# First phase's page scores behind the decay sums, four value sets in the last projection, and the first norm's last tiles in banks and a buffer of their own

## The chip, the cores and the metric

One core of a Trainium2 chip runs the whole program: one inference step of a two-layer decoder trunk. The metric is the device time of one execution in microseconds (us), as the median of several runs. The profile is one further execution, taken by the hardware profiler.

## What is computed

1024 prompt tokens and 8 decode samples, 1024 features, everything in float32 (each product is made of three matmuls on split operands, `x_hi*w_hi + x_lo*w_hi + x_hi*w_lo`):

```
x1 = LN(a*x  + (1+gate)*chunk_mlp(x*(1+scale)+shift))          # layer 0
k, v, logf = x1 @ kv_w + kv_b ;  c = cumsum(log_sigmoid(logf))   # "decay sums"
y  = LN(a*x1 + (1+gate)*(softmax(q k^T/8 + c_q - c_k) v * silu(z)) @ w_out)   # layer 1
```

Each of the 8 samples attends to 512 past positions, which lie in 4 pages of 128 positions in `cache_k` and `cache_v` (32 pages in all, found by `page_table`), and to its own new key. Its scores come from the key pages, its output from the value pages.

## The kernel before, in words

Every engine runs a list that is written out by hand; semaphores (`wait_ge`) tie the lists together. SP and POOL also issue the DMAs. A DMA that waits holds up all that stands behind it in its engine's list. The SP's transfers go through queue q1, those of POOL through q0.

**The first norm.** Layer 0's result `rT` (features x tokens) is turned tile by tile, 128 tokens at a time (tiles 0 to 7). For tile t, PE turns it into PSUM (`ln_forward`, line 1985, pair 1 of banks for every tile), DVE makes its statistics (`layer_norm_stats`), ACT writes the normed tile `xhat` (L816), PE turns that back (`ln_backward`, L1992, into pair 2 + t%2), DVE and ACT each write half of it into `x1f` (`x1_back` L1318, `x1_back_act` L827; two buffers, t%2), POOL issues a store of it to `scr_x` (L589), ACT rounds it to `x_hi` (L836) and POOL subtracts, `x_lo = x1f - x_hi` (L592). Buffer t%2 may be written again only when its store has landed. Tiles 5, 6 and 7 stand behind the last block of layer 0's output projection. In between, PE runs the product for `logf` (`token_step` on bank 1, and then on bank 2 for tokens 512 to 1023, which needs all eight `x_lo`) and the first half of the first key block (bank 0).

**The decay sums.** DVE scans `logf` into `fc` (L1575, L1576). POOL stores it (`scr_c`, L613), waits for it and for the store of `logf` itself (`f_out`, L611), and loads it back as rows that are repeated on all partitions, `ckb` (`load_c`, L617). DVE's `peak` (L1479) needs `ckb`, and PE's third `peak` of a phase needs DVE's first.

**Phases.** Eight phases j = 0 to 7, two heads each: PE interleaves the attention of heads 2j, 2j+1 (`peak`, `scores` L2169, `values` L2188) with the projections for phase j+1 (`steps`, lines 1826 to 1828). In phases 0 to 5 DVE also makes the page scores of the 8 samples in four pieces c (`score_mul(j, c)` L1432 and `score_sum(j, c)` L1440, from `kpb` and `qb`). SP issues for each phase, in `load_phase`: `load_swapped` (KX, 4 DMAs), the next phase's weights (`load_b`, into `raw`), the key pages (`load_keys`, `kpb`), the sample queries (`put_q` writes 4 bytes per element to `scr_q`, `get_q` reads it back as `qb`), and the scores (`put_scores`).

**The last projection and the end.** Eight blocks b in two halves each (n = 2b + half). `decode_values(n)` multiplies value set n (4 pages, 2 MB) on PE (L2344), and POOL's `load_values(n)` fetches it into a slot of `pages` (4 DMAs of 512 KB, L691). Slots 0 and 1 are free early, slots 2 and 3 lie under operands of the projection. Then the second norm runs over 8 tiles: `ln_forward(t)` on PE, `layer_norm_stats(t)` and `finish(t)` on DVE (L1786 and L1790 into `yo`, two buffers; `finish(t)` for t >= 2 waits until the store of t-2 has landed), stores `y_out` by SP (L528). The samples' path goes through `mask_o` (DVE, L1734), a PE product (L2384), `gated_s` (DVE), the product with `fsw` (PE, L2392; the 4 MB of `fsw` are loaded by SP at L524, ahead of all `y_out` in SP's list), `fs_row` (DVE, L1806), a fold (PE, L2398), `residual_s`, two sums over features (`sample_sum`), and `norm_out`; the store `ys_out` of that is the last thing of all.

## Time and profile before

| | |
|---|---|
| median of 3 runs (lowest to highest) | 1765.38 us (1764.94 to 1765.78) |
| the profiled execution: its own time | 1757.93 us |
| its span, from first to last record | 1756.3 us |
| PE busy | 1643.2 us, 94% of the span |
| DVE, ACT, POOL busy | 58%, 36%, 24% |
| granted PE clock, mean | 0.975 of full speed |

The profiled execution was 7.45 us below the median of the runs shown. Times inside the program are counted from the start of the span. A wait in brackets is the idle time of the engine just before an instruction, with what ended it. The busy share of PE is an average; where PE waits is read from its waits and from the timelines.

### The profile page before, as it was taken

To read this page: it belongs to the slowest core of one execution; us is meant where nothing else is said; L and a number is where in the kernel's file an instruction comes from. 1 tells how busy PE (TensorE), PEld (TensorE's weight loads), DVE (VectorE), ACT (ScalarE), POOL (GpSimd) and SP (SyncE) were. 2 spreads that over 40 slices of the span, in tenths; PEclk is the share of its full clock that TensorE was granted. 3 is DMA by queue.
4 is the path that set the end of the run, shared out by engine and by line. 5 is a ranking of instruction groups with operands and counts; after the bars stand their busy time and mean duration, and the time that the engine had idled before them with its cause. 6 is when DMAs were issued, how large, how long until landed. Compare 5 with 4: busy or idle time off the path is not lost.

```text
span 1756.3 us, 27853 instructions
## 1 busy us (share of the span) xinstructions
PE 1643.2 (94%) x10080; PEld 1428.1 (81%) x10080; DVE 1011.8 (58%) x1571; ACT 623.8 (36%) x980; POOL 420.2 (24%) x414
## 2 busy tenths in 40 slices
PE   6999989999999998999887999999999999979965
PEld 4899989999999997999865777787777777757742
DVE  3433353433433437225566888879797977689436
ACT  2222122112112117224442646463636455463221
POOL 0240010110111100001221626262534344250020
PEclk8999999999999998999998999999999999999987
DMA  8481112222222221324324242424333221243474
GB/s 363 158 315 36 48 61 93 77 72 95 72 72 96 73 71 56 109 92 154 118 72 135 84 113 69 120 74 118 97 95 97 84 72 72 73 133 132 159 283 194
DMA packets 85777, 197.90 MB, mean 113 GB/s; under 512 B 16898, under 2 KB 47234, under 8 KB 83922
## 3 DMA queue, kind: packets, MB, share of 16 engines
q1 hardware_dynamic: 73154, 141.97, 24.9%
q0 software_dynamic: 12560, 55.10, 8.9%
q8 instruction: 38, 0.62, 0.2%
q14 instruction: 25, 0.20, 0.0%
HBM read 171.31 MB, written 34.39 MB: 117 GB/s over the span
## 4 chain that ended last, share of the span: by engine, by line
PE 77%; DVE 9%; issue 5%; DMA 3%; ACT 3%; POOL 2%; POOLq 0%; SPq 0%; DVEq 0%; ACTq 0%
PE bank L1826 20%; PE bank L1827 19%; PE bank L1828 19%; PE bank L2188 2%; PE bank L2142 2%; PE bank L2190 2%; PE bank L2189 2%; PE bank L1961 2%; PE bank L2170 1%; DVE bank L1479 1%; PE bank L2169 1%; POOL p_lo L640 1%; DMA pages<-cache_v 1%; PE bank L1941 1%; PE bank L2045 1%
## 5 line engine op out<-in xcount | busy, mean ns | idle before, releaser
L1826 PE MATMUL bank<-h_hi,w_lo 128*128 128x344 f32 x1152 | 374.5, 325 | 9.9 <-DVE h_lo L1125 8.7
L1827 PE MATMUL bank<-h_lo,w_hi 128*128 128x344 f32 x1152 | 369.0, 320 | 0.0
L1828 PE MATMUL bank<-h_hi,w_hi 128*128 128x344 f32 x1152 | 368.7, 320 | 0.0
L640 POOL TENSOR_TENSOR p_lo<-parg,p_hi 128x512 fp32r<-128x512 f32 (+1 forms) x192 | 226.8, 1199 | 161.4 <-ACT p_hi L966 160.7
L1826 PEld LDWEIGHTS bank<-h_hi,w_lo 128*128 128x128 f32 x1152 | 217.7, 189 | 14.8 <-issue 12.2
L1826 PE MATMUL bank<-x_hi,w_lo 128*128 128x512 f32 x528 | 222.1, 421 | 6.6 <-POOL x_lo L592 6.5
L1827 PEld LDWEIGHTS bank<-h_lo,w_hi 128*128 128x128 f32 x1152 | 217.8, 189 | 0.2 <-issue 0.2
L1828 PEld LDWEIGHTS bank<-h_hi,w_hi 128*128 128x128 f32 x1152 | 217.7, 189 | 0.0
L1827 PE MATMUL bank<-x_lo,w_hi 128*128 128x512 f32 x528 | 209.7, 397 | 0.0
L1828 PE MATMUL bank<-x_hi,w_hi 128*128 128x512 f32 x528 | 209.6, 397 | 0.0
L1826 PE MATMUL bank<-y_hi,w_lo 128*128 128x320 f32 (+2 forms) x512 | 177.4, 346 | 13.7 <-DVE w_lo L1083 6.5
L1083 DVE TENSOR_TENSOR w_lo<-raw,w_hi 128x1024 fp32r<-128x1024 f32 x105 | 144.7, 1378 | 75.5 <-ACT w_hi L718 74.1
L1827 PE MATMUL bank<-y_lo,w_hi 128*128 128x320 f32 (+2 forms) x512 | 174.6, 341 | 0.0
L1828 PE MATMUL bank<-y_hi,w_hi 128*128 128x320 f32 (+2 forms) x512 | 174.2, 340 | 0.0
L964 ACT ACTIVATE parg<-parg 128x512 f32<-128x512 f32 (+1 forms) x192 | 99.0, 515 | 114.5 <-DVE parg L1521 114.3
L565 POOL TENSOR_TENSOR vcur<-V,vr 128x1024 f32<-128x1024 f32 x16 | 31.1, 1944 | 439.8 <-PE bank L1961 317.9
L718 ACT ACTIVATE w_hi<-raw 128x1024 fp32r<-128x1024 f32 x105 | 111.1, 1058 | 54.6 <-PE bank L1828 51.7
L1521 DVE SCALAR_TENSOR_TENSOR parg<-bank,cph,mb 128x512 f32<-128x512 f32 (+1 forms) x192 | 108.8, 607 | 35.1 <-PE bank L2170 30.9
L1826 PEld LDWEIGHTS bank<-x_hi,w_lo 128*128 128x128 f32 x528 | 101.3, 192 | 29.2 <-issue 7.6
L1828 PEld LDWEIGHTS bank<-x_hi,w_hi 128*128 128x128 f32 x528 | 100.3, 190 | 24.0
L1826 PEld LDWEIGHTS bank<-y_hi,w_lo 128*128 128x128 f32 x512 | 97.5, 190 | 24.5 <-issue 13.5
L1827 PEld LDWEIGHTS bank<-x_lo,w_hi 128*128 128x128 f32 x528 | 100.9, 191 | 15.1
(300 smaller groups left out, 2622.5 us busy)
## 6 DMA issues: line engine op xcount, KB each, us to landing
raw<-units SPq DMA_DIRECT2D x121, 512.0 KB, 3.5
scr_k<-cache_k POOLq DMA_DIRECT2D x32, 512.0 KB, 5.4
ada_ring<-w_ada SPq DMA_DIRECT2D x32, 512.0 KB, 3.3
pages<-cache_v POOLq DMA_DIRECT2D x32, 512.0 KB, 6.1
kpb<-scr_k SPq DMA_DIRECT2D x24, 512.0 KB, 4.1
ada_first<-w_ada SPq DMA_DIRECT2D x8, 1024.0 KB, 14.8
KX<-KA SPq DMA_DIRECT2D x32, 256.0 KB, 6.9
ckb<-scr_c POOLq DMA_DIRECT2D x16, 512.0 KB, 4.7
```

The lines of the kernel that those rows point to most:

```text
L640: g.tensor_tensor(p_lo[:, r, off:HALF], parg[:, r, off:HALF], p_hi[:, r, off:HALF].bitcast(F32), ALU.subtract).then_inc(S("p_ready"), 1)
L718: A(w_hi[:, slot, :, :], raw[:, slot, :, :], ACT.Copy).then_inc(S("hi_ready"), 1)
L964: A(parg[:, r, off:HALF], parg[:, r, off:HALF], ACT.Exp, scale=SCALE).then_inc(S("p_exp"), 1)
L1083: v.tensor_tensor(w_lo[:, slot, :, :], raw[:, slot, :, :], w_hi[:, slot, :, :].bitcast(F32), ALU.subtract)\
L1521: v.scalar_tensor_tensor(parg[:, r, off:HALF], ps[1 + slot][:, h, off:HALF], cph[:, h, kt:kt + 1], mb[:, h, off:HALF], ALU.add, ALU.add).t ...
L1826: mm(out, lhs_lo, rhs_hi, start=first, stop=False)
L1827: mm(out, lhs_hi, rhs_lo, start=False, stop=False)
L1828: return mm(out, lhs_hi, rhs_hi, start=False, stop=last)
L1961: last = mm(pair(3)[:, t * P:(t + 1) * P], vcur[:, t, :], rhs, start=True, stop=True)
L2142: mm(out[:, ks], QA[:, h, qs], KA[:, h, ks], start=True, stop=ks.stop < (qt + 1) * P)
L2188: mm(out, v_block(0, kt, h), p_hi[:, r, off:HALF], start=kt == 0, stop=False)
L2189: mm(out, v_block(0, kt, h), p_lo[:, r, off:HALF], start=False, stop=False)
```

## The change

Four edits, none of which adds or removes arithmetic:

1. *First norm, tiles 5 to 7.* `ln_forward(6)` goes to pair 2 of banks and no longer waits for `xhat` of tile 5; it stands right behind `ln_forward(5)`. Tile 7's `x1f` gets a third buffer (`x1_columns`), so it waits for no store. DVE's statistics of 6 and 7 and ACT's parts move up. On POOL `x_low(6)` stands ahead of the stores of 6 and 7, and tile 7's `x_lo` is made by DVE.
2. *First phase's page scores.* On SP, `load_query(0)` and `load_keys(0, 0)` go from ahead of `load_phase(0)` to behind its `load_swapped` and first `load_b`, and wait for both `ckb` loads. On DVE, the score pieces of phase 0 come one place later each: piece 0 stands where piece 1 stood, and piece 3 behind `kq_low(1, 0)`.
3. *Value sets.* Sets 4 and 5 use slots 0 and 1, sets 6 and 7 slots 2 and 3. Four sets (n = 9, 10, 13, 14) instead of two (n = 11, 12) are multiplied inside the last projection. SP's `fsw` loads wait until sets 6 and 7 have landed.
4. *Order at the end.* PE turns tiles 4 to 7 behind the values and between the samples' steps; DVE's list follows.

```diff
@@ sync
             def load_phase(j, scored):
                 load_swapped(j)
                 load_b(j + 1, 0)
+                if isinstance(j, int) and j == 0:
+                    for h in range(2):
+                        sp.wait_ge(S(f"ckb_in{h}"), 16)
+                    load_query(0)
+                    sp.wait_ge(S("pages_in0"), MOVED)
+                    load_keys(0, 0)
                 load_b(j + 1, 1)
                 load_keys(j, 1)
...
             sp.wait_ge(S("ln1_back"), TT)
-            load_query(0)
-            sp.wait_ge(S("pages_in0"), MOVED)
-            load_keys(0, 0)
             load_phase(0, True)
...
             sp.wait_ge(S("lo_ready"), U_FS)
+            sp.wait_ge(S("pages_in2"), 32 * NP)
             for b in range(KB):
                 sp.dma_start(fsw[:, b, :, :], units[U_FA - WB + b, :, :, :]).then_inc(S("fsw_in"), 16)
@@ gpsimd
+            for t in range(TT - 2):
+                store_x(t)
+                x_low(t)
+            x_low(TT - 2)
+            store_x(TT - 2)
+            store_x(TT - 1)
...
             for n in range(NS):
                 if n < 2:
                     pool.wait_ge(S("pages_used"), SCORED - 4 + 4 * n)
-                elif n < 4:
+                elif n < 6:
                     pool.wait_ge(S("pages_used"), SCORED + n - 1)
-                elif n == 4:
+                elif n == 6:
                     pool.wait_ge(S("fa_mm"), 2 * KB)
-                elif n >= 6:
-                    pool.wait_ge(S("pages_used"), SCORED + n - 3)
                 load_values(n)
@@ scalar
-            back1_act(5)
+            x1_back_act(5)
             norm1_act(7)
+            x1_hi(5)
             back1_act(6)
             back1_act(7)
@@ vector
             layer_norm_stats(5, 0)
+            layer_norm_stats(6, 0)
             split_lo(0, 0)
-            layer_norm_stats(6, 0)
+            layer_norm_stats(7, 0)
             x1_back(5)
...
             x1_back(7)
+            dve.wait_ge(S("x1_hi"), TT)
+            v.tensor_tensor(x_lo[:, :, T - P:T], x1f[:, :, x1_columns(TT - 1)], x_hi[:, :, T - P:T].bitcast(F32), ALU.subtract)\
+                .then_inc(S("x1_ready"), 1)
...
                 if more:
                     kq_low(j + 1, 0)
+                    if late_keys:
+                        score_mul(j, 3)
+                        score_sum(j, 3)
...
             layer_norm_stats(1, TT)
-            for t in range(2, 5):
-                finish(t - 2)
-                layer_norm_stats(t, TT)
+            finish(0)
+            layer_norm_stats(2, TT)
+            finish(1)
+            layer_norm_stats(3, TT)
+            finish(2)
+            mask_o()
+            layer_norm_stats(4, TT)
             finish(3)
-            mask_o()
+            gated_s()
             layer_norm_stats(5, TT)
             finish(4)
-            gated_s()
...
@@ tensor
             ln_forward(5, rT, 0)
+            ln_forward(6, rT, 0)
             pe.wait_ge(S("lo_ready"), U_F + 1)
             pe.wait_ge(S("x1_ready"), TT // 2)
             for k in range(KB // 2):
                 token_step(bank(1), 0, 0, k)
-            ln_forward(6, rT, 0)
+            ln_forward(7, rT, 0)
             ln_backward(5)
             for k in range(KB // 2, KB):
                 last = token_step(bank(1), 0, 0, k)
             last.then_inc(S("f_mm"), 1)
-            ln_forward(7, rT, 0)
+            ln_backward(6)
             pe.wait_ge(S("lo_ready"), U_B + 1)
-            for k in range(KB // 2):
+            for k in range(2):
                 token_step(bank(0), 1, 0, k)
-            ln_backward(6)
-            for k in range(KB // 2, KB):
+            ln_backward(7)
+            for k in range(2, KB):
                 last = token_step(bank(0), 1, 0, k)
             last.then_inc(S("mm"), 1)
-            ln_backward(7)
             pe.wait_ge(S("x1_ready"), TT)
```

The order on ACT around the first norm's last three tiles (`xhat`: the normed tile; `x1f`: ACT's half of the tile turned back; `x_hi`: the rounded tile; `bankNM` is the pair read). Before:

```order
L812 ACTIVATE lr_163<-lr_163 128x1
L816 ACTIVATE xhat_80<-bank23,lnm_164,lr_163 128x8x128
L812 ACTIVATE lr_163<-lr_163 128x1
L816 ACTIVATE xhat_80<-bank23,lnm_164,lr_163 128x8x128
L827 ACTIVATE x1f_81<-bank67,cols_132 128x128 x4
L836 ACTIVATE x_hi_82<-x1f_81 128x8x128
L812 ACTIVATE lr_163<-lr_163 128x1
L816 ACTIVATE xhat_80<-bank23,lnm_164,lr_163 128x8x128
L827 ACTIVATE x1f_81<-bank45,cols_132 128x128 x4
```

And now:

```order
L830 ACTIVATE lr_163<-lr_163 128x1
L834 ACTIVATE xhat_80<-bank23,lnm_164,lr_163 128x8x128
L830 ACTIVATE lr_163<-lr_163 128x1
L834 ACTIVATE xhat_80<-bank45,lnm_164,lr_163 128x8x128
L845 ACTIVATE x1f_81<-bank67,cols_132 128x128 x4
L830 ACTIVATE lr_163<-lr_163 128x1
L834 ACTIVATE xhat_80<-bank23,lnm_164,lr_163 128x8x128
L854 ACTIVATE x_hi_82<-x1f_81 128x8x128
L845 ACTIVATE x1f_81<-bank45,cols_132 128x128 x4
```

Tile 6 is now read from the other pair (`bank45`), and tile 7's `xhat` has moved ahead of tile 5's `x_hi`.

SP's list at the start of phase 0 (`raw`: weights; `scr_q`, `qb`: the samples' queries out and back; `kpb`: key pages; `KX`: the swapped keys). Before:

```order
L427 DMA scr_q<-kqvzS 128x8x1
L431 DMA qb<-scr_q 128x1024
L453 DMA kpb<-scr_k 128x8x128
L420 DMA KX<-KA 64x1024 x4
L344 DMA raw<-units 128x1024 x2
L453 DMA kpb<-scr_k 128x8x128
L344 DMA raw<-units 128x1024
```

And now:

```order
L424 DMA KX<-KA 64x1024 x4
L348 DMA raw<-units 128x1024
L431 DMA scr_q<-kqvzS 128x8x1
L435 DMA qb<-scr_q 128x1024
L457 DMA kpb<-scr_k 128x8x128
L348 DMA raw<-units 128x1024
L457 DMA kpb<-scr_k 128x8x128
```

`scr_q`, `qb` and the first `kpb` have moved behind `KX` and the first `raw`; everything below them keeps its order.

PE's list behind the last matmul of the last projection (`r2T` turned: `ln_forward`; `pages`: a value set; `omask`, `fsw`, `fs_row`, `red`: the samples' steps). Before:

```order
L1985 MATMUL bank01<-ident_133,r2T_104 128x128 x8
L2344 MATMUL bank67<-pages_105,PZ_110 32x512 x8
L1985 MATMUL bank23<-ident_133,r2T_104 128x128 x8
L2344 MATMUL bank67<-pages_105,PZ_110 32x512 x16
L2384 MATMUL bank45<-maskp_171,omask_122 128x8 x8
L1985 MATMUL bank01<-ident_133,r2T_104 128x128 x8
L2392 MATMUL bank67<-fsw_128,oS_178 8x512 x16
L1985 MATMUL bank23<-ident_133,r2T_104 128x128 x8
L2398 MATMUL bank45<-fold4_170,fs_row_129 128x8 x8
L1923 MATMUL bank45<-red_151,ones_135 128x8 x2
```

And now:

```order
L2391 MATMUL bank67<-pages_105,PZ_110 32x512 x16
L2435 MATMUL bank45<-maskp_171,omask_122 128x8 x8
L2031 MATMUL bank01<-ident_133,r2T_104 128x128 x8
L2443 MATMUL bank67<-fsw_128,oS_178 8x512 x16
L2031 MATMUL bank23<-ident_133,r2T_104 128x128 x8
L2449 MATMUL bank45<-fold4_170,fs_row_129 128x8 x8
L2031 MATMUL bank01<-ident_133,r2T_104 128x128 x8
L1965 MATMUL bank45<-red_151,ones_135 128x8
L2031 MATMUL bank23<-ident_133,r2T_104 128x128 x8
L1965 MATMUL bank45<-red_151,ones_135 128x8
```

Before, two `ln_forward` (tiles 6 and 7) stood among the samples' steps; now four do (tiles 4 to 7), and the last one stands between the two sums.

## Rows read from the trace of the kernel before

**Rows 1.** PE's waits, whole program: us in total, times, longest us

```profile
PE bank L2344 <- DMA pages<-cache_v: 19.2, 2, 15.9
```

**Rows 2.** Timeline of PE and POOL, first norm's end: start us, us

```profile
898.46 0.79 PE L1826 MATMUL bank<-x_hi,w_lo 128*128 128x512 f32 x1 [6.51 <-POOL x_lo L592]
...
896.05 2.36 POOL L592 TENSOR_TENSOR x_lo<-x1f,x_hi 128x1024 fp32r<-128x1024 f32 x1
```

**Rows 3.** The chain that ended last, PE behind that wait: start us, us

```profile
903.52 0.43 PE bank L1827
...
904.50 0.23 PE bank L1827
```

**Rows 4.** Timeline of SP's DMA issues at the start of phase 0

```profile
919.21 0.41 SPq L427 DMA_DIRECT2D scr_q<-kqvzS  x1
929.96 0.34 SPq L431 DMA_DIRECT2D qb<-scr_q  x1
...
930.96 3.06 SPq L420 DMA_DIRECT2D KX<-KA  x4
```

**Rows 5.** Timeline of POOL in the same stretch

```profile
924.52 0.51 POOL L613 DMA_DIRECT2D scr_c<-fc  x1 [2.55 <-DVE fc L1576]
...
931.56 1.13 POOL L617 DMA_DIRECT2D ckb<-scr_c  x2
```

**Rows 6.** DMA issues of the whole program: count, KB each, median us to landing

```profile
f_out<-fp POOLq DMA_DIRECT2D x1, 64.5 KB, 9.0
vn_out<-vnS POOLq DMA_DIRECT2D x1, 64.0 KB, 1.9
scr_c<-fc POOLq DMA_DIRECT2D x1, 64.0 KB, 6.1
...
ckb<-scr_c POOLq DMA_DIRECT2D x16, 512.0 KB, 4.7
```

**Rows 7.** Timeline of PE: third peak and first scores of phases 0 and 1

```profile
946.03 0.69 PE L2142 MATMUL bank<-KA,QA 128*128 128x384 f32 x1 [9.90 <-DVE nmin L1479]
...
969.32 0.39 PE L2169 MATMUL bank<-QA,KA 128*128 128x512 f32 x1
...
1029.19 0.34 PE L2142 MATMUL bank<-KA,QA 128*128 128x384 f32 x1
...
1050.42 0.39 PE L2169 MATMUL bank<-QA,KA 128*128 128x512 f32 x1
```

**Rows 8.** Landing times of all 24 `kpb` loads, and DVE at phase 0's end

```profile
DMA to landing us min/median/max: 3.7/4.1/8.7
...
1014.23 1.21 DVE L1440 TENSOR_REDUCE sst<-kpb 128x16 f32<-128x1024 f32 x1
...
1023.22 0.29 DVE L1364 COPY samp<-bank 128x128 f32<-128x128 f32 x1 [3.51 <-PE bank L2045]
```

**Rows 9.** PE in the last projection and at the end

```profile
1669.99 1.92 PE L2344 MATMUL bank<-pages,PZ 128*32 128x512 f32 x16
...
1733.22 1.74 PE L1985 MATMUL bank<-ident,r2T 128*128 128x128 f32 x8
1736.20 5.62 PE L2392 MATMUL bank<-fsw,oS 128*8 128x512 f32 x32 [1.24 <-DVE oS L1740]
```

**Rows 10.** DVE at the end

```profile
1716.66 1.23 DVE L1790 TENSOR_TENSOR yo<-xh,b_row 128x1024 f32<-128x1024 f32 x1 [10.29 <-DMA y_out<-yo]
...
1742.88 1.30 DVE L1299 BATCH_NORM_STATS2 lst<-bank 128x6 f32<-128x512 f32 x2 [0.29 <-PE bank L1985]
...
1745.15 1.22 DVE L1786 TENSOR_TENSOR xh<-xh,g_row 128x1024 f32<-128x1024 f32 x1
```

**Rows 11.** Tile `yo`: landing times of its eight stores

```profile
DMA to landing us min/median/max: 2.6/3.6/18.2
```

**Rows 12.** Windows: busy us of PE, PEld, DVE, ACT, POOL; PE clock, DMA share, GB/s

```profile
1692.00:1714.00 22.00, 5.89 (x49) 2.54 (x48) 12.82 (x28) 5.62 (x8) 7.52 (x14) 0.74 1.02 398
1631.00:1640.10 9.10, 9.10 (x46) 7.54 (x45) 5.62 (x10) 2.83 (x4) 2.15 (x4) 1.00 0.73 249
```

More of the change, by code:

```diff
@@ L306, in ln_pair, with x1_columns @@
         def ln_pair(t, n0):
-            return 1 if n0 == 0 else t % 2
+            return (2 if t == TT - 2 else 1) if n0 == 0 else t % 2
+        def x1_columns(t):
+            return columns(2 if t == TT - 1 else t % 2)
         def out_parts(bb):
@@ L584, in _, with store_x, x_low @@
             pool.dma_start(vn_out, vnS[:, :, :]).then_inc(S("vn_out"), 16)
[L586 removed]
+            def store_x(t):
                 pool.wait_ge(S("x1f_ready"), t + 1)
                 pool.wait_ge(S("x1f_upper"), t + 1)
[L589 removed]
+                pool.dma_start(scr_x[:, :, t * P:(t + 1) * P].rearrange("k p t -> p k t"), x1f[:, :, x1_columns(t)])\
                     .then_inc(S(f"scr_x_out{t % 2}"), 16)
+            def x_low(t):
                 pool.wait_ge(S("x1_hi"), t + 1)
[L592 removed]
+                g.tensor_tensor(x_lo[:, :, t * P:(t + 1) * P], x1f[:, :, x1_columns(t)],
                                 x_hi[:, :, t * P:(t + 1) * P].bitcast(F32), ALU.subtract).then_inc(S("x1_ready"), 1)
+            for t in range(TT - 2):
[4 more added lines that the diff above has]
+            store_x(TT - 1)
             def scale(j, q, k0, k1):
@@ L826, in x1_back_act @@
                 for k in range(KB // 2, KB):
-                    last = A(x1f[:, k, columns(t % 2)], pair(2 + t % 2)[:, k * P:(k + 1) * P], ACT.Identity,
+                    last = A(x1f[:, k, x1_columns(t)], pair(2 + t % 2)[:, k * P:(k + 1) * P], ACT.Identity,
                              bias=col("ln_b", k), scale=col("ln_g", k))
@@ L835, in x1_hi @@
                     act.wait_ge(S("hl_used"), U_AGAIN if t == 0 else U_F)
-                A(x_hi[:, :, t * P:(t + 1) * P], x1f[:, :, columns(t % 2)], ACT.Copy).then_inc(S("x1_hi"), 1)
+                A(x_hi[:, :, t * P:(t + 1) * P], x1f[:, :, x1_columns(t)], ACT.Copy).then_inc(S("x1_hi"), 1)
             def split_hi(j, q):
@@ L1317, in x1_back @@
                 for k in range(KB // 2):
-                    last = v.tensor_scalar(x1f[:, k, columns(t % 2)], pair(2 + t % 2)[:, k * P:(k + 1) * P],
+                    last = v.tensor_scalar(x1f[:, k, x1_columns(t)], pair(2 + t % 2)[:, k * P:(k + 1) * P],
                                            col("ln_g", k), col("ln_b", k), ALU.mult, ALU.add)
@@ L1584, in phase @@
                 later = not isinstance(j, int) or j > 0
+                late_keys = keys and not later
+                keys = keys and later
                 take_samples(j, 2)
@@ L1625, in phase @@
                     invert(j - 1, 1, 1)
+                if late_keys:
+                    score_sum(j, 0)
                 if keys:
@@ L1643, in phase @@
                 divide_o(j, 0)
+                if late_keys:
+                    score_sum(j, 1)
                 if keys:
@@ L1655, in phase @@
                 exponents(j, 10)
+                if late_keys:
+                    score_sum(j, 2)
                 if keys:
@@ L1806, in _ @@
                 v.tensor_copy(fs_row[:, h * 512:(h + 1) * 512], bank(6 + h)).then_inc(S("fs_row"), 1)
-            layer_norm_stats(7, TT)
-            finish(6)
+            layer_norm_stats(6, TT)
+            finish(5)
             dve.wait_ge(S("fs_used"), 3)
@@ L1813, in _ @@
             norm_sum(rS[:, :, :], KB)
-            finish(7)
+            layer_norm_stats(7, TT)
+            finish(6)
             norm_square(3, rS[:, :, :], KB, rS[:, :, :])
             norm_var(3)
+            finish(7)
             norm_out(3, KB, "ln_g", KB, "ln_b", rS[:, :, :]).then_inc(S("ys_ready"), 1)
@@ L1980, in ln_forward @@
             def ln_forward(t, src, n0):
-                wait(pe, S("ln_hat"), n0 + t - (1 if n0 else 0))
+                if n0 == 0 and t == TT - 2:
+                    pe.wait_ge(S("x1f_ready"), t - 1)
+                    pe.wait_ge(S("x1f_upper"), t - 1)
+                else:
+                    wait(pe, S("ln_hat"), n0 + t - 1 if n0 or t == TT - 1 else t)
                 if n0 == 0 and t in (0, TE // P):
@@ L1990, in ln_backward @@
                 wait(pe, S("x1f_ready"), t - 1)
+                wait(pe, S("x1f_upper"), t - 1)
                 for k in range(KB):
@@ L2376, in _ @@
             ln_forward(1, r2T, TT)
-            for n in range(2, 6):
+            for n in range(4, 6):
                 decode_values(n)
-                ln_forward(n, r2T, TT)
+                ln_forward(n - 2, r2T, TT)
             decode_values(6)
@@ L2385, in _ @@
             last.then_inc(S("d_o"), 1)
-            ln_forward(6, r2T, TT)
+            ln_forward(4, r2T, TT)
             pe.wait_ge(S("d_step"), 5)
@@ L2393, in _ @@
                 last.then_inc(S("fs_used"), 1)
-            ln_forward(7, r2T, TT)
+            ln_forward(5, r2T, TT)
             for h in range(2):
@@ L2399, in _ @@
             last.then_inc(S("fs_used"), 1)
+            ln_forward(6, r2T, TT)
             sample_sum(3, 0)
+            ln_forward(7, r2T, TT)
             sample_sum(3, 1)
```

30 lines of the change are left out of this document (17 added, 13 removed).

## The prediction

> **What bounds the kernel now.** I read PE's waits first, since PE is busy 94% of the span. The three largest that the diff touches are two with 19.2 us together on value pages at the end [rows 1], one of 9.9 us in phase 0 [rows 7] and one of 6.5 us at the first norm's end [rows 2]. Then I read the timelines around each place, engine by engine, to see what stands behind the releaser that is named, then the DMA issues with their landing times, and last the windows at the end. The reader should see that the first two waits lie in a program that PE bounds on both sides, so what they lose goes straight off the end, while from 1692 us on PE is no longer the bound: in the next 22 us it is busy for 5.9, DVE for 12.8, and the DMAs all the time [rows 12]. I take all times from the profiled execution and keep its clock of before; a sum of gains is applied to its 1756.3 us and then to the median, which lies 7.45 us above that execution's own time.
>
> **First norm.** Nothing is added but 1.2 us on DVE: `x_lo` of tile 7, which POOL made in 2.36 us at 896.05 [rows 2]; DVE's operation on two such tiles takes 1.22 [rows 10]. The chain that PE waits for runs through one pair of banks: tile 7 could not be turned until tile 6 was normed, and behind its `xhat` two POOL subtractions of 2.4 us with a store's issue (0.9) behind each other followed. Now tiles 5 and 6 are turned back to back at 873 to 877; `xhat` 6 comes at about 880, tile 7 is turned at about 880, its statistics (2.3) stand on DVE behind `split_lo` at 881 to 883.6, and `xhat` 7 ends at about 885. ACT is then the longest list: `x_hi` 5, `x1f` 6, `x_hi` 6, `x1f` 7, `x_hi` 7, some 1.05 and 1.5 each, from 885 to 891.3; DVE's `x_lo` ends at 892.6. PE's own work up to the wait is unchanged and ends at 891.95. So 0.7 us of the 6.5 stay. Behind the old wait 13 matmuls ran at 0.43 instead of 0.23 us [rows 3]: the granted clock had fallen to 1.2 GHz in the wait. With 0.7 us of idle time I expect no fall, 2.6 us more. Against it stands 0.4 us for the first `sample_sum`, which now waits for DVE behind the added subtraction. **Gain 7.8 us**; bounds 5.6 (the clock falls all the same) and 9.1 (all of it).
>
> **Phase 0.** The 9.9 us are a wait for `ckb`. Removed from its way is more than the 1 MB of `qb` and `kpb`. SP issued `scr_q` at 919.21 and saw it land only before 929.96 [rows 4]: 1024 elements of 4 bytes. In that time POOL issued `f_out` and `scr_c`, which took 9.0 and 6.1 us to land, where a store of the same 64 KB (`vn_out`) took 1.9 [rows 6]. `scr_c` landed at 924.52 + 6.05 = 930.57, 0.6 us behind `scr_q`, and only then could POOL go on to `ckb` at 931.56 [rows 5]. I read that as: the two small stores were held by `scr_q`. The Trainium skill ("DMA: Bandwidth & Descriptors", Queues, rings and completion order) says that a DMA's semaphore increment lands only after every earlier write of that DMA engine, across its queues; the trace agrees, and without that rule the two stores would end no earlier and the term would be the 6.2 us below.
>
> Now `scr_q` is issued behind `ckb`. `scr_c`, issued at 924.52 [rows 5], lands at 926.5 (by `vn_out`), the memsets end at 927.5, and `ckb` is issued 4 us earlier, ahead of `KX`, and lands in its median 4.7 us [rows 6], at 932.5 and 933.5. PE gets to its third `peak` at 936.1, DVE to its first a little ahead of that, so nothing is waited for. What that is worth is read from phase 1, which has the same PE list without the wait: from third `peak` to first `scores` 21.2 us, in phase 0 33.2 from PE's arrival at 936.1 [rows 7]. The 12.0 are the 9.9 and the slow clock behind it. I take **11.8 us**. The lower bound: `scr_c` still lands at 930.5; then only fewer bytes are ahead of `ckb`. 1 MB at the 249 GB/s of [rows 12], the slower of two rates, is 4.2 us, and `KX`, which stood behind `scr_q`'s wait until 930.96 [rows 4], is out of the way 2 us earlier: 6.2 us.
>
> What moves behind it on SP: `scr_q` 934 to 945, `qb` and the first `kpb` by 950, used at 967. Each later `kpb` of phase 0 comes one place later, and with it the `raw` that SP issues behind it. The last `kpb` can be asked for when `score_sum(0, 2)` ends, 1015.4; with 4.1 us it lands at 1019.6, when DVE is through with `kq_low(1, 0)`, and piece 3 (2.45 us) fills the 3.5 us in which DVE waited for PE until 1023.22 [rows 8]. Phase 1's `qb`, `kpb`, `KX` and one `raw` go 8.6 us later, into some 10 us of room. I cost this at nothing; if the cover is gone, see the second rival.
>
> **The end.** Two more value sets in the projection take 1.87 us each on PE [rows 9], so it ends 3.7 us later, at 1692.2. Only sets 6 and 7 are then left: POOL issues 8 DMAs from 1693.4, 1.15 us apart. Four such DMAs alone took 9 us from first issue to last landing [rows 12]; eight I put at 15, landing at 1708.4 (bounds 1706 and 1710). PE's values end at 1712. The old 15.9 us wait is gone, but what decides is DVE. Its `finish(2)` waits for the store of tile 0, and `mask_o` stands behind it. SP issues `fsw` only once the pages have landed, and the store behind `fsw`. In the trace that store was issued at 1698.3 and took 18.2 us [rows 11], 2.5 us longer than the last `fsw`: one queue, served in order. At 398 GB/s for both queues [rows 12], 4 MB of `fsw` and 0.5 of the store take 11.6 us, with 2.3 of latency: DVE resumes at R = 1722.3, where before it did at 1716.7 after 10.3 us of idle time [rows 10].
>
> From R, by rows 9 and 10: `yo`, `mask_o` 2.4; PE `omask` at the low clock, to which it has fallen in 10 us of idle time, 3.6, and `ln_forward(4)` 1.75; a tile on DVE costs 2.27 (statistics) + 2.4 (finish), so `gated_s` at R+12.7. PE: `fsw` product 5.6, `ln_forward(5)` 1.1 to R+19.4. DVE: tile 4.7, copies 1.3; PE fold and `ln_forward(6)` 2.0 to R+27.5. DVE: tile 4.7 and 1.3; PE sum and `ln_forward(7)` 2.3 to R+35.7. DVE: tile 4.7, squares 1.2, sum 0.7, `finish(7)` 2.4; its store 2.6 [rows 11], `ys_out` 1.9: R+49.7, **1772.0** against 1756.3. In the old list tiles 6 and 7 were turned while DVE worked; now DVE idles three times behind PE's sample steps (7, 2 and 2.3 us). Loss 15.7 us; bounds 12.5 (R 1719.5 and no slow clock) and 19 (R 1725).
>
> **Sum:** 15.7 - 7.8 - 11.8 = -3.9: span 1752.4, median 1765.38 - 3.9 = **1761.5 us**. 0.2% (3.5 us) is about what a measurement can tell from no change, so this lies just beyond it. With the terms' bounds the case runs from 1757 to 1769.
>
> **Rivals.** *The store is not held by `fsw`* (0.15): it lands 3.6 us after an issue at 1713. For it: the median of the stores [rows 11]. Against: the 18.2. R = 1716.6, 5.7 less: 1755.8. *SP comes late into phase 1* (0.12), the slower one: if the last `kpb` of phase 0 takes 8.7 us [rows 8], it lands at 1024.3, DVE waits for it ahead of `samp` and `kq_low(1, 1)`, and PE's first `peak` of phase 1, which needs that result at once, waits 3.5 us, with 2.2 for the clock; `raw` for the phase after, behind 2.5 MB in SP's queue, costs 2 more. It decides from a landing later than 1020.7. 1769.2. Against: in this stretch nothing else is in flight. *`scr_c` is slow by itself* (0.15): a load and a store that end together may be chance, `ckb` gains 6.2 and not 11.8: 1767.1. Against: `vn_out`. Forecast 0.55; 0.03 for what I don't see.
>
> **How the numbers follow.** Faster: half of the forecast, the first rival, a little of the rest: 0.48. Same: 0.4 of the forecast, two thirds of the third rival: 0.36. Slower: the second rival, and the top of the others: 0.16. The range 1754 to 1769.5 holds the forecast and most of each rival.
>
> **What would show it.** No `x_lo` wait over 1.5 us before bank 2's product, and `x_lo` of tile 7 on DVE; `scr_c` landing in under 3 us; no `nmin` wait in phase 0; 20.5 to 22 us from third `peak` to first `scores`; no PE wait at phase 1's first `peak`. At the end: values done by 1712 less 19.6; DVE waiting some 12 us on `y_out`; three DVE waits on PE behind `gated_s`. I am wrong if that DVE wait is short, if `scr_c` still takes 6 us, or if phase 1 starts with a wait.

## The result and the profile after

The changed kernel takes **1767.21 us**, median of 20 runs (1764.17 to 1769.98), beside 1762.94 for the kernel before in as many: ratio 1.0025, 95% interval 1.0018 to 1.0033. It is 4.4 us slower, where 3.9 us faster was forecast. The profiled execution of the changed kernel has a span of 1764.1 us (its own time is 1765.59), 7.8 more than the 1756.3 of before; its mean granted clock is 0.973 against 0.975. Of these 7.8 us, 3.4 are in the choice of the executions and not in the change: the one of before lay 5.0 us below its median of 20 runs, that of the change 1.6 below its own.

First norm and phase 0, PE's timeline at the wait of [rows 2], then POOL's behind it (start, duration, in brackets idle time and releaser):

```profile
892.15 0.50 PE L1868 MATMUL bank<-x_hi,w_lo 128*128 128x512 f32 x1 [0.91 <-DVE x_lo L1573]
```

```profile
916.89 0.51 POOL L633 DMA_DIRECT2D scr_c<-fc  x1 [2.54 <-DVE fc L1598]
919.12 0.99 POOL L665 MEMSET Vst<- 128x512 f32 x2 [1.72 <-DMA scr_c<-fc]
920.05 1.12 POOL L637 DMA_DIRECT2D ckb<-scr_c  x2
```

The 6.51 us have become 0.91. `scr_c` is issued 7.6 us earlier than in [rows 5], and lands in 2.2 us instead of 6.1, so that `ckb` goes out 11.5 us earlier. The wait of 9.9 us [rows 7] is gone. DVE's first gating of a phase (`gate_o`) is a mark that both kernels have; in phases 0 and 1, before and then now (DVE's timelines):

```profile
988.89 0.68 DVE L1532 TENSOR_TENSOR y2T<-bank,y2T 64x512 f32<-64x512 f32 x1 [1.06 <-PE bank L2190]
...
1070.46 0.68 DVE L1532 TENSOR_TENSOR y2T<-bank,y2T 64x512 f32 x1 [1.04 <-PE bank L2190]
```

```profile
969.92 0.68 DVE L1552 TENSOR_TENSOR y2T<-bank,y2T 64x512 f32<-64x512 f32 x1 [1.06 <-PE bank L2237]
...
1055.22 0.68 DVE L1552 TENSOR_TENSOR y2T<-bank,y2T 64x512 f32 x1 [1.04 <-PE bank L2237]
```

In phase 0 **19.0 us** are gained up to there. In phase 1 only 15.2 are left, at the last one 14.2, at the first tile turned for the second norm 10.0 (1680.14 against 1690.10), and at the end of the span the gain is a loss of 7.8. The last stretch is read from one window each, from the first turned tile to the end, of before and of after (length, busy us of PE, PEld, DVE, ACT, POOL, then PE's clock, the DMAs' share and GB/s):

```profile
1690.10:1756.30 66.20, 32.85 (x228) 16.30 (x228) 39.97 (x83) 11.97 (x18) 8.21 (x16) 0.75 0.65 255
```

```profile
1680.10:1764.10 84.00, 34.33 (x196) 19.82 (x196) 39.89 (x83) 12.02 (x18) 3.96 (x8) 0.65 0.42 160
```

DVE has the same 83 operations and the same 39.9 us of work. The stretch is 17.8 us longer because DVE idles 44 us in it and not 26. Where, PE's and DVE's timelines tell:

```profile
1695.38 5.28 PE L2391 MATMUL bank<-pages,PZ 128*32 128x512 f32 x32 [6.43 <-DMA pages<-cache_v]
1713.32 3.58 PE L2435 MATMUL bank<-maskp,omask 128*128 128x8 f32 x16 [12.65 <-DVE omask L1773]
1716.76 1.95 PE L2031 MATMUL bank<-ident,r2T 128*128 128x128 f32 x8
1723.68 6.47 PE L2443 MATMUL bank<-fsw,oS 128*8 128x512 f32 x32 [4.98 <-DVE oS L1779]
1730.08 1.09 PE L2031 MATMUL bank<-ident,r2T 128*128 128x128 f32 x8
1736.62 3.58 PE L2449 MATMUL bank<-fold,fs_row 128*128 128x8 f32 x16 [5.44 <-DVE fs_row L1846]
1740.06 1.95 PE L2031 MATMUL bank<-ident,r2T 128*128 128x128 f32 x8
```

```profile
1710.91 1.23 DVE L1829 TENSOR_TENSOR yo<-xh,b_row 128x1024 f32<-128x1024 f32 x1 [14.49 <-DMA y_out<-yo]
1712.05 1.22 DVE L1773 TENSOR_TENSOR omask<-bank,hm 128x1024 f32<-128x1024 f32 x1
1718.74 1.29 DVE L1318 BATCH_NORM_STATS2 lst<-bank 128x6 f32<-128x512 f32 x2 [5.48 <-PE bank L2031]
1723.41 0.22 DVE L1779 SCALAR_TENSOR_TENSOR oS<-bank,sq 128x64 f32<-128x64 f32 x1
1731.21 1.29 DVE L1318 BATCH_NORM_STATS2 lst<-bank 128x6 f32<-128x512 f32 x2 [7.59 <-PE bank L2031]
1742.04 1.29 DVE L1318 BATCH_NORM_STATS2 lst<-bank 128x6 f32<-128x512 f32 x2 [4.88 <-PE bank L2031]
1750.44 1.29 DVE L1318 BATCH_NORM_STATS2 lst<-bank 128x6 f32<-128x512 f32 x2 [2.49 <-PE bank L2031]
```

Of PE's 19.2 us of waiting for pages [rows 1] 6.4 are left. But the values are done at 1700.7 and DVE multiplies them with the mask (`mask_o`, which writes `omask`) only at 1712.05, because that stands in its list behind `finish(2)`, and `finish(2)` behind the store of tile 0. Behind it PE and DVE take turns: four waits of DVE for PE, 5.5, 7.6, 4.9 and 2.5 us, where before, behind `mask_o`, one of 0.5 us and the one of 0.29 [rows 10] stood. (Before, DVE had waited 5.2 us for the values ahead of `mask_o`.)

### The profile page after: what moved, and what is told of

The parts are those of the page before. It is cut to its first block, busy times and chain, and to the rows that moved or that the text cites. A ratio compares the mean times of both kernels' runs of the same rounds, so it can differ in the third digit from the quotient of the medians.

```text
span 1764.1 us, 27851 instructions
## 1 busy us (share of the span) xinstructions
PE 1645.3 (93%) x10080; PEld 1428.4 (81%) x10080; DVE 1010.4 (57%) x1572; ACT 624.0 (35%) x980; POOL 417.3 (24%) x413
## 4 chain that ended last, share of the span: by engine, by line
PE 75%; DVE 11%; issue 5%; ACT 3%; DMA 3%; POOL 2%; SPq 0%; POOLq 0%; DVEq 0%; ACTq 0%
PE bank L1868 19%; PE bank L1869 18%; PE bank L1870 18%; PE bank L2235 2%; PE bank L2003 2%; DVE bank L1499 2%; PE bank L2189 2%; PE bank L2236 2%; PE bank L2237 2%; PE bank L2217 1%; PE bank L2216 1%; POOL p_lo L660 1%; PE bank L1983 1%; PE bank L2092 1%; DMA raw<-units 1%
## 5 line engine op out<-in xcount | busy, mean ns | idle before, releaser
L1868 PEld LDWEIGHTS bank<-h_hi,w_lo 128*128 128x128 f32 x1152 | 217.2, 189 | 15.2 <-issue 11.2
```

Of the source, the lines that this page charges most:

```text
L1868: mm(out, lhs_lo, rhs_hi, start=first, stop=False)
```

## The experiments

All medians are of runs side by side with the kernel before; its own median lay between 1761.8 and 1764.0 in the four groups of runs.

| kernel | median us | ratio to before, 95% | first turned tile to end, us |
|---|---|---|---|
| before | 1762.94 | 1 | 66.2 |
| the change | 1767.21 | 1.0025 (1.0018 to 1.0033) | 84.0 |
| e3, first norm alone | 1756.55 | 0.9963 (0.9949 to 0.9977) | 67.7 |
| e4, phase 0 alone | 1750.74 | 0.9938 (0.9924 to 0.9952) | 66.4 |
| e1, both, end as before | 1744.01 | 0.9896 (0.9881 to 0.9911) | 66.3 |
| e2, end alone | 1782.89 | 1.0113 (1.0098 to 1.0129) | 82.6 |
| e7, `scr_q` early | 1775.18 | 1.0070 (1.0052 to 1.0087) | 82.6 |
| e5, weights ahead | 1765.72 | 1.0019 (1.0008 to 1.0030) | 82.2 |
| e12, mask ahead | 1760.57 | 0.9991 (0.9980 to 1.0003) | 75.2 |
| e8, stores first | 1755.35 | 0.9963 (0.9949 to 0.9977) | 73.4 |
| e9, four sets, old list | 1744.86 | 0.9900 (0.9883 to 0.9917) | 63.2 |
| e10, the two together | 1733.35 | 0.9847 (0.9825 to 0.9869) | 52.4 |
| e11, two sets, stores first | 1744.47 | 0.9897 (0.9877 to 0.9916) | 65.3 |
| e13, and pages before fsw | 1745.84 | 0.9897 (0.9882 to 0.9911) | 66.0 |

### The parts alone

e1 takes of the change the hunks of the first norm and of phase 0 and leaves those of the value sets and the end as before; e2 the reverse; e3 and e4 take one of the first two. In short, for e1:

```diff
-        VALUE_SLOT = (0, 1, 0, 1, 0, 1, 2, 3)
+        VALUE_SLOT = (0, 1, 0, 1, 2, 3, 0, 1)
...
-            sp.wait_ge(S("pages_in2"), 32 * NP)
...
-            ln_forward(4, r2T, TT)
+            ln_forward(6, r2T, TT)
```

for e2, and with the first norm's hunks kept for e3:

```diff
+            load_query(0)
+            sp.wait_ge(S("pages_in0"), MOVED)
+            load_keys(0, 0)
             load_phase(0, True)
...
-                late_keys = keys and not later
-                keys = keys and later
```

and for e4 (and e2) the first norm as before:

```diff
-            return (2 if t == TT - 2 else 1) if n0 == 0 else t % 2
+            return 1 if n0 == 0 else t % 2
```

> The first norm and phase 0 as changed, value sets and end lists as before. Theory: the two gains are 7.6 and 11.4 us, as the trace of the change shows up to the first exponents, and 3.7 us of them are lost again at the start of phase 1, where a weight load that SP issued 0.6 us ahead of the query's 4-byte store landed after 11.8 us; the whole loss of the change lies at the end. Then this kernel is 15.3 us below before: ratio 0.9913, and its profile shows DVE waiting about 2 us each twice behind POOL's scaling and ACT's split near 1012 and 1026 us. Rival (the prediction's own terms): nothing is lost at phase 1's start, 19.6 us below before, ratio 0.9889. Second rival: gains in the first half are taken back at the projection by the weights' loads, whatever the end does; then under 10 us, ratio above 0.994.

> Only the four value sets in the projection and the new lists of the end; first norm and phase 0 as before. Theory: the loss is all here, 4.3 us in the projection and 17.8 behind it, 22 us in all: ratio 1.0125. Rival (the prediction's own term): 15.7 us, ratio 1.0089; the rest of the loss would then come from the end meeting an earlier first half.

> Only the first norm's last tiles in other banks and a buffer of their own. Theory: 7.6 us below before (ratio 0.9957), since nothing behind it has room that would take it up, and x_lo's wait is about 1 us. Rival: PE comes earlier to phase 0's peaks while the decay sums do not, because the query's store holds them until the same time; then the gain is under 4 us (ratio above 0.9977) and the wait for nmin is above 12 us instead of 9.9.

> Only phase 0's page scores behind the decay sums, with what SP issues moved. Theory: 11.4 us gained at phase 0's peaks and 3.7 given back at phase 1's start: 7.7 us below before, ratio 0.9956, with scr_c landing in under 3 us, no wait for nmin over 1 us, and phase 1's first weight load landing after 10 us or more. Rival: the loss at phase 1's start comes only together with the earlier first norm; then 11.4 us, ratio 0.9935.

By their ratios the first norm gives 6.5 us, phase 0 10.9, both together **18.3**, and the end alone loses **19.9**. So the whole loss lies at the end: e1 beats both kernels. The two halves would add up to a loss of 1.6 us, beside the 4.4 measured; with intervals of about 2.6 us on each of them, that is no sign that they act on each other. e3's rival falls with its trace: PE waits 10.1 us for `nmin`, about as before, and `scr_c` still takes 6.2 us to land, but both come earlier by what the norm gained (`scr_c` is issued 7.6 us earlier, counted from the end of the last part of the program that both kernels share). e4 gains 11.3 at `gate_o` of phase 0 by the same count and keeps it: nothing is lost there at phase 1's start.

That last point is where my reading of the trace of the change was too narrow. Its 3.7 us at phase 1's start are 0.1 in e4's trace and 1.3 in e1's, although the weight load in question landed nearly as late there (9.7 and 10.8 us behind its issue). Up to the last projection e1 and the change are the same program, so the size varies from one execution to the next.

### What held the decay sums

```diff
             sp.wait_ge(S("ln1_back"), TT)
+            put_q(0)
             load_phase(0, True)
...
-                    load_query(0)
+                    sp.wait_ge(S("scr_q"), 16)
+                    settle(sp, S("settled"))
+                    get_q(0, qb)
```

> The change, with one thing of before back: the query's 4 KB store of phase 0 is issued right behind the first norm, ahead of the decay sums' store; the 1 MB of loads behind it (qb, kpb) stay where the change puts them. Theory (the prediction's reading): the store of 1024 elements of 4 bytes holds the landing of the two small stores, scr_c lands after 5 to 6 us instead of 2.2, ckb is issued some 3.5 us later, PE waits for nmin again, and the time is 3 to 5.5 us above the change. Rival: what held the decay sums before were the bytes of qb and kpb; then scr_c lands in 2.2 us and the time is that of the change.

The 4 KB store alone brings the wait back. POOL's and PE's timelines of this kernel:

```profile
918.91 0.51 POOL L636 DMA_DIRECT2D scr_c<-fc  x1 [2.54 <-DVE fc L1601]
925.64 0.99 POOL L668 MEMSET Vst<- 128x512 f32 x2 [6.23 <-DMA scr_c<-fc]
926.58 1.12 POOL L640 DMA_DIRECT2D ckb<-scr_c  x2
```

and its landing times of `scr_c` and, in the second line, of the first two `ckb`:

```profile
DMA to landing us min/median/max: 6.7/6.7/6.7
...
DMA to landing us min/median/max: 8.9/9.5/10.2
```

`scr_c` takes 6.7 us beside `scr_q` and 2.2 without it, in the change and in e4; `f_out` takes 9.4 and 2.2. That is shown, and the rival (the bytes of `qb` and `kpb`) falls. The Trainium skill ("DMA: Bandwidth & Descriptors", Queues, rings and completion order) gives the rule that fits, an increment that lands only after every earlier write of its DMA engine, across queues; the runs show its effect on two stores, not the rule itself. My price of 3 to 5.5 us was too low: e7 is 7.9 above the change (1.0070 against 1.0025). `ckb`, issued 4.5 us later against its `scr_c`, now goes out behind `KX` (922.68) and lands after 9.5 us, the mean of two, instead of 6.1, so DVE waits 5.4 us for it, and PE 7.4 for `nmin`. A hold of 4.5 us on a small store cost nearly twice that: the other 3.4 us are `ckb`'s own, which now had `KX` ahead of it.

### Phase 1's start

```diff
                 load_keys(j, 2)
-                load_keys(j, 3)
-                load_b(j + 1, 3)
-                if scored:
-                    load_query(j + 1)
+                if isinstance(j, int) and j == 0:
+                    load_b(1, 3)
+                    put_q(1)
+                    load_keys(0, 3)
...
+                    sp.wait_ge(S("scr_q"), 32)
+                    wait(sp, S("qk_prod"), 4)
+                    get_q(1, qb)
```

> The change, but in phase 0 SP issues the last weight load and the query's store ahead of the last page of keys. In the profiles so far that load was issued 0.6 us ahead of the query's store and landed after 11.8, 10.8 and 9.7 us; behind it phase 1 began 3.7, 1.2 and 0.1 us late. Theory: the store's 4-byte elements hold the landing of what is in flight with it; with the load 12 us ahead of the store it lands in about 4 us, no wait of POOL's scaling on it over 1 us is left in this stretch, and the time is 1 to 3.7 us lower than with the change. Rival: the load takes long because of the bytes ahead of it in SP's queue; then it lands no faster, and the time is that of the change.

The first half came out: issued 4.3 us ahead of the store, the weight load landed in 4.6 us (4.7 in the kernel before, where it was 4.3 us ahead as well; 11.8 in the change), and POOL's scaling does not wait for it. The second did not: the ratio, 1.0019, is not to be told from 1.0025. The late landing moved to the load that is now behind the store, the last page of keys:

```profile
1004.73 1.23 DVE L1461 TENSOR_TENSOR kpb<-kpb,qb 128x1024 f32<-128x1024 f32 x1 [2.55 <-DMA kpb<-scr_k]
```

`kpb` took 6.6 us where it took 4.0 before, and this trace still loses 2.7 us between `gate_o` of phase 0 and that of phase 1. Over the eleven profiles that have the new phase 0 that loss is 0.1 to 3.7 us, in eight of them between 2.5 and 3.7, with no fixed relation to the weight load's landing (9.7 us in e4 with 0.1 lost, 9.7 in e8 with 3.6).

PE's waits between the two marks say where it goes. Before and in e4 none is longer than 0.35 us. In the change there is one of 2.09 us, at the end of the chain that the late load starts: POOL's scaling `w_sc`, ACT's split `w_hi`, DVE's `w_lo`, and behind that DVE's `md`, which PE multiplies next (POOL, DVE and PE):

```profile
1009.12 1.90 POOL L624 TENSOR_TENSOR w_sc<-raw,one_p 128x1024 f32<-128x1024 f32 x1 [7.66 <-DMA raw<-units]
1012.23 1.23 DVE L1107 TENSOR_TENSOR w_lo<-w_sc,w_hi 128x1024 fp32r<-128x1024 f32 x1 [1.99 <-ACT w_hi L863]
1016.59 1.10 PE L2198 MATMUL bank<-md,ones 128*128 128x512 f32 x2 [2.09 <-DVE md L1508]
```

In seven others PE waits 0.9 to 1.5 us for DVE's `QA` at its first `peak` of phase 1. In the kernel that is called e10 below (POOL, DVE and PE):

```profile
999.64 1.43 POOL L666 TENSOR_TENSOR p_lo<-parg,p_hi 128x128 fp32r<-128x128 f32 x1
1005.24 1.91 POOL L630 TENSOR_TENSOR w_sc<-raw,one_p 128x1024 f32<-128x1024 f32 x1 [4.17 <-DMA raw<-units]
1004.17 4.06 DVE L1435 TENSOR_TENSOR QA<-qf,QA 64x1024 fp32r<-64x1024 f32 x2
1008.36 0.32 PE L2192 MATMUL bank<-KA,QA 128*128 128x128 f32 x1 [1.49 <-DVE QA L1435]
```

The two operations that write `QA` take 4.06 us here and 2.47 in the change: the second one begins while POOL's `w_sc` runs, and lasts 2.81 us instead of 1.22. So it is in five profiles (e7, e10 to e13); in e9 the first one takes 2.18. A little earlier POOL's `p_lo` takes 1.43 us instead of 0.45 in the eight profiles in which DVE's product with the last `kpb` began ahead of it, and PE waits 0.84 us for it. In the change and in e4 that product began 0.05 to 0.1 us behind `p_lo`, and in e5 2 us behind; there `p_lo` took 0.45. These waits order the loss: none in e4 (0.1 us lost), 0.84 in e1 (1.3), 0.84 and 0.87 in e9 (1.9), 0.84 and 1.49 in e10 to e13 (2.6 each). In e7 and e8 (3.7 and 3.6) about 1 us more goes than the long waits hold. What varies is thus which operations of DVE and POOL meet, by tenths of a us, now that the last page's scores stand in this place. That is read from traces; no run moved one of these operations alone.

### The end: the store, the mask, the list

Three edits to the change, each alone. e8 moves two stores ahead of `fsw`, with the helper `store_y` around the two lines that are taken out below:

```diff
             sp.wait_ge(S("lo_ready"), U_FS)
+            store_y(0)
+            store_y(1)
             sp.wait_ge(S("pages_in2"), 32 * NP)
...
-            for t in range(TT):
-                sp.wait_ge(S("yo_ready"), t + 1)
-                sp.dma_start(y_out[t * P:(t + 1) * P, :], yo[:, t % 2, :]).then_inc(S(f"y_out{t % 2}"), 16)
+            for t in range(2, TT):
+                store_y(t)
```

e12 moves one line of DVE's list:

```diff
+            mask_o()
             finish(2)
-            mask_o()
```

e9 keeps the four value sets and takes both end lists from before:

```diff
-            for n in range(4, 6):
-                decode_values(n)
-                ln_forward(n - 2, r2T, TT)
+            for n in range(2, 6):
+                if n < 4:
+                    decode_values(n + 2)
+                ln_forward(n, r2T, TT)
...
-            ln_forward(4, r2T, TT)
+            ln_forward(6, r2T, TT)
             pe.wait_ge(S("d_step"), 5)
```

> The change, with the stores of output tiles 0 and 1 issued ahead of SP's wait for the last pages, and so ahead of the 4 MB of fsw; the other six behind it as before. Theory: finish(2) no longer waits (14.5 us in the trace of the change), mask_o then waits only for the values, which end 2.5 us later than 1700.7 since the stores take part of the bandwidth; it starts at about 1703 where it did at 1712, and all behind it goes 9 us earlier: 1758. Rival: the chain of PE and DVE behind it takes up what is gained, since fsw lands later and gated_s then waits; under 4 us.

> The change with one line of DVE's end list moved: mask_o ahead of finish(2), so that it does not stand behind the wait for the store of tile 0. Stores, fsw and PE's list stay. Theory (a wait counts for what is queued behind it): mask_o starts at about 1701 us in the profile, PE's mask product and the turning of tile 4 lie within DVE's wait, gated_s comes 6 us behind the end of that wait instead of 12.5, and the time is 6 us lower than with the change: 1761. Rival: the store's late landing alone sets the end, since fsw lands with it, and PE idles in the sample steps as before; then within 2 us of the change.

> The change with its four value sets in the projection, but with PE's and DVE's end lists as before (tiles 2 to 5 turned before the last values, tile 6 behind the mask's product). SP's wait for the pages ahead of fsw stays. Theory: half of the loss is the list, not the value sets: finish(2) still waits for the store until about 1711 (profile coordinates of the change), and from there the old list takes 39.6 us where the new one takes 53.2: 13.6 us less, 1753.6. It then still lies above the version without the four sets (1744). Rival: the list costs little by itself and the store behind fsw is all: within 4 us of the change.

In e8 DVE's wait for the store is gone, and `mask_o` waits for the values (DVE's timeline):

```profile
1706.07 1.22 DVE L1779 TENSOR_TENSOR omask<-bank,hm 128x1024 f32<-128x1024 f32 x1 [5.02 <-PE bank L2397]
1711.63 1.30 DVE L1324 BATCH_NORM_STATS2 lst<-bank 128x6 f32<-128x512 f32 x2 [4.35 <-PE bank L2037]
1724.06 1.30 DVE L1324 BATCH_NORM_STATS2 lst<-bank 128x6 f32<-128x512 f32 x2 [7.54 <-PE bank L2037]
```

It comes 22.6 us behind the first turned tile (31.9 in the change), and the stretch is 10.6 shorter: 11 us by the ratio, 9 expected. The turns behind it are as they were (7.54 again). e12 brings 6 us by the ratio, as expected. Its wait for the store is still 7.26 us, but PE's product with `omask` and the turning of tile 4 lie inside it, and `gated_s` follows 5.8 us behind the wait instead of 12.5. So what the late store cost was partly what stood behind it in DVE's list.

e9 is where I was furthest off: 22 us below the change by the ratios, not 13.6. The wait for the store is unchanged; DVE's timeline, with what follows it:

```profile
1716.15 1.23 DVE L1829 TENSOR_TENSOR yo<-xh,b_row 128x1024 f32<-128x1024 f32 x1 [14.28 <-DMA y_out<-yo]
...
1727.74 0.22 DVE L1779 SCALAR_TENSOR_TENSOR oS<-bank,sq 128x64 f32<-128x64 f32 x1
1728.64 1.29 DVE L1318 BATCH_NORM_STATS2 lst<-bank 128x6 f32<-128x512 f32 x2 [0.68 <-PE bank L2028]
...
1735.30 1.30 DVE L1318 BATCH_NORM_STATS2 lst<-bank 128x6 f32<-128x512 f32 x2 [0.29 <-PE bank L2028]
```

From the end of that wait to the end of the span it takes 32.7 us, the change 53.2. DVE finds its next tile turned each time (0.68 and 0.29 instead of 7.59 and 4.88), and PE's fold takes 1.85 us instead of 3.58. PE's clock stands behind the busy times of the five engines in a window over the fold, of e9 and of the change:

```profile
1734.20:1737.00 2.80, 2.75 (x28) 2.66 (x24) 2.32 (x5) 0.00 (x0) 0.00 (x0) 1.00 0.49 193
```

```profile
1736.60:1742.00 5.40, 5.38 (x24) 4.98 (x24) 0.56 (x1) 0.00 (x0) 0.00 (x0) 0.50 0.25 100
```

That is 2.4 and 1.2 GHz; ahead of the fold PE had idled 5.4 us in the change and not at all in e9. So **the list is the loss**, all of it: with the list of before, four sets are no worse than two (e9 and e1: 0.9900 and 0.9896). PE's and DVE's lists were put back together; no run tells them apart.

### Together, and what the four sets are worth

e10 is e9 with e8's stores. e11 is e1 (two sets in the projection) with the same stores; e13 adds to it SP's wait for the last pages:

```diff
             store_y(0)
             store_y(1)
+            sp.wait_ge(S("pages_in0"), MOVED + 48 * NP)
+            sp.wait_ge(S("pages_in1"), 48 * NP)
```

> Four value sets in the projection, the end lists of before, and the stores of tiles 0 and 1 ahead of fsw: the two improvements of the last runs together. Theory: without the store's wait mask_o starts when the values are done, 22.5 us behind the first turned tile (it was 36.4 with the old list and the late store), so 13.9 us below the version with the old list alone: 1731, some 30 us below before. Rival: the two overlap, since with the old list DVE is the bound from the first tile on; then at most 5 us below it, 1740.

> Two value sets in the projection and the end as before, with the new first norm and phase 0, and the stores of tiles 0 and 1 ahead of fsw. It tells what the four sets are worth once the store is out of the way. Here fsw is also issued 13 us later, behind the second tile, so that the last four sets of pages have the bandwidth for themselves: 8 MB at 398 GB/s are 21 us from 1677, 1698 instead of 1714. Theory: mask_o starts at about 1703 where it did at 1716 with the late store, and the time is 1733, within 5 us of the version with four sets, because the two more sets cost PE 4.2 us ahead of the end and save about as much of the pages' wait. Rival: the four sets are what lets the end be short; then this one stays at 1740 or above.

> The version with two value sets in the projection and the two stores ahead of fsw, with SP's wait for the last pages ahead of fsw added, so that the order of the transfers is that of the version with four sets: stores, pages, fsw. It tells whether the 11 us between those two (1744.5 and 1733.4) come from the value sets or from fsw taking the pages' bandwidth. Theory: from fsw. The 16 page loads are issued from 1675.9 to 1694.9 and land by about 1700 instead of 1711.9, mask_o starts at 1704, and from there the version with four sets takes 28.6 us: 1733 in the profile, a median of 1735. Rival: from the sets; four sets of pages still to come at 1676 hold the end whatever else flows, the last land past 1706, and the median stays above 1740.

e10 is **1733.35 us, 27 us below before** by its ratio (0.9847; 29 by the medians), the best of all. Its last stretch, its `mask_o`, its wait for a store and its `fsw`, then those of e13:

```profile
1678.90:1731.30 52.40, 28.85 (x196) 15.84 (x196) 39.77 (x83) 11.97 (x18) 3.91 (x8) 0.74 0.67 256
...
1702.74 1.23 DVE L1779 TENSOR_TENSOR omask<-bank,hm 128x1024 f32<-128x1024 f32 x1 [1.68 <-PE bank L2394]
1710.38 1.22 DVE L1835 TENSOR_TENSOR yo<-xh,b_row 128x1024 f32<-128x1024 f32 x1 [3.01 <-DMA y_out<-yo]
...
1695.61 3.98 SPq L539 DMA_DIRECT2D fsw<-units  x8
```

```profile
1675.00:1741.00 66.00, 33.24 (x228) 16.18 (x228) 39.96 (x83) 11.96 (x18) 8.20 (x16) 0.75 0.67 255
...
1705.52 1.22 DVE L1782 TENSOR_TENSOR omask<-bank,hm 128x1024 f32<-128x1024 f32 x1 [4.98 <-PE bank L2397]
1718.82 1.22 DVE L1838 TENSOR_TENSOR yo<-xh,b_row 128x1024 f32<-128x1024 f32 x1 [8.68 <-DMA y_out<-yo]
...
1703.55 3.72 SPq L540 DMA_DIRECT2D fsw<-units  x8
```

Of 52.4 us DVE is busy for 39.8. e11 and e13 refute what I expected of them and settle the question in favour of the rival: with two sets, 8 MB of pages are still to come when the norm begins. In e11 `fsw` shares the bandwidth, the last set is used at 1711.9 and DVE waits 13.8 us for it. In e13 the pages come earlier (used from 1703.5), but `fsw` goes out 7.9 us later than in e10, though its first tile is turned 3.9 us earlier, and the store of tile 2 behind it makes DVE wait 8.7 us. Either way DVE's longest wait is one for transfers, 13.8 and 8.7 us, where e10 has one of 3.0. The mean rates are nearly the same, 256 GB/s over 52.4 us with four sets and 255 over 66 with two, and well under the 398 of [rows 12]: DVE waits for single transfers that come late, not for a rate that is full throughout. The two extra sets take 4 MB out of this stretch, and by the ratios e10 is 8.8 us faster than either of e11 and e13. The store's move needs the sets as well: with two sets it brings nothing (e1 0.9896, e11 and e13 0.9897), with four 9.3 us by the ratios (e9 to e10). The value sets were a good edit, made worthless by the list around them.

## Why the prediction was wrong

The forecast was a gain of 3.9 us; the profiles show a loss of 7.8, 11.7 away from it, and the medians a loss of 4.4. That the median of 1767.2 still lies within the stated 1754 to 1769.5 is no merit: none of the rivals brought it there, but terms that all erred towards too short a time. Step by step, in the profiles, whose pair overstates the loss by 3.4 us:

- **First norm**, 7.8 forecast: 7.6. The wait left is 0.91 us, the first matmul behind it takes 0.50 us where it took 0.79 [rows 2], so the clock did not fall; PE waits 0.97 us for DVE's `hS` ahead of its product of `x1S` and `samp`; 0.4 had been put down for a wait behind the added subtraction, at the first `sample_sum`, where none is seen.
- **Phase 0**, 11.8 forecast: 11.4. `scr_c` landed in 2.2 us, and e7 shows that it was `scr_q` that held it. The third rival is refuted. The lower bound was too high: with the hold back (e7), 2.3 us of this gain are left at `gate_o` and not 6.2.
- **SP behind it**, costed at nothing: 3.7 us in the trace of the change, 0.1 to 3.7 in others. "Phase 1's `qb`, `kpb`, `KX` and one `raw` go 8.6 us later, into some 10 us of room" is a step that failed. They went 10 us later (`KX` at 1011.15, against 1020.14 less 19.0), and the room was not there. The second rival named the place. In the change its carrier, a late `kpb` with a wait of PE at the first `peak`, is not seen: DVE waited 0.4 us for the `kpb`, the `raw` ahead of `scr_q` came after 11.8 us, and PE waited 2.09 us for `md`. In seven of the other profiles PE does wait at that `peak`, 0.9 to 1.5 us for `QA`, mostly because DVE and POOL met. That DVE's added scores would lengthen operations of POOL, and POOL's those of DVE, was in no term. About 1 us more goes in the last two phases, and I cannot say to what.
- **The projection**, 3.7 forecast for two more sets: 4.2 in the trace of the change, from the last `gate_o` to the first turned tile. The seven variants with four sets lie 5.5 to 5.9 us above before there, but three with two sets (e3, e11, e13) 1.5 to 1.6 above it as well. In all ten the granted clock fell behind a wait of PE for `ktok` of 2.6 to 2.9 us (0.83 over the 10 us that start 20 us behind the last `gate_o`); in before, the change, e1 and e4 it stayed at 1.00, behind waits as long. So the sets cost 4.2, and 1.6 us come and go.
- **The end**, forecast at 78.2 us from the first turned tile (1693.8 to 1772.0): 84.0. **This is the step that failed, and alone it turns the sign**, from -3.9 to +1.9. The mechanism was right in each link: DVE waits on `y_out` (14.5 us, 12 forecast), `mask_o` behind it, and then three waits of DVE on PE behind `gated_s` (7.6, 4.9 and 2.5; 7, 2 and 2.3 forecast). Two sizes were off. R came 30.8 us behind the first tile and not 28.5: the pages were 0.6 later, and between 1696 and 1711 the queues moved 348 GB/s, not the 398 of [rows 12], a stretch in which pages and `fsw` overlapped. And "PE fold and `ln_forward(6)` 2.0" took 4.9 from DVE's last copy to its statistics: I had PE at the full clock there, but it had idled 5.4 us and the granted clock was 0.50, so the fold took 3.58 us and the turning 1.95, where they take 1.85 and 1.09 in e9 (2.9 together, so that the term was short even at the full clock). From R to the end that made 53.2 us, 49.7 forecast.

The sum of the differences is 0.2 + 0.4 + 3.7 + 1.1 + 0.5 + 5.8, or 11.7. No single term is absurd, but each errs on the same side.

The first rival (the store not held by `fsw`) is refuted: it landed 12.2 us behind its issue in the change, and e8, which takes it out of `fsw`'s way, gains 11 us.

## What to carry to other kernels

When a stretch is no longer bound by the engine that bounds the program, write down the busiest engine's work in it (DVE's 39.8 to 40.0 us here, in every version) and judge an edit by how much idle time it leaves between: the list that turned tiles only between the sample steps cost 22 us, and one line or two stores moved brought 6 and 11 of them back. A small store in the way of others, or a load queued ahead of a store that something waits for, is cheaper to move than to hide. And an edit that measures as a loss may hold a part that is worth keeping: the four value sets gain nothing by themselves and 8.8 us once the list and the stores are right.
